# Recurrent layer: the two token tiles go through the doubling levels half a level apart, with the state's products in ten pieces

## The reference, cut to what matters

```python
def wkv7_scan(r, w, k, v, kk, a):          # heads H = 32, N = 64
    def step(state, inp):
        r_t, w_t, k_t, v_t, kk_t, a_t = inp
        sa = jnp.einsum('bhvk,bhk->bhv', state, -kk_t)
        state = (state * w_t[:, :, None, :]
                 + sa[..., None] * (kk_t * a_t)[:, :, None, :]
                 + v_t[..., None] * k_t[:, :, None, :])
        return state, jnp.einsum('bhvk,bhk->bhv', state, r_t)
    ...
    _, out = lax.scan(step, state0, xs)
# odd_layer, around it
    o = wkv7_scan(r, decay, k, v, kk, a)
    o = ((o - mean) * lax.rsqrt(var + GN_EPS)).reshape(B_, S, D) * gn_w + gn_b
    bonus = jnp.sum(r * k * r_k, axis=-1, keepdims=True) * v
    o = (o + bonus.reshape(B_, S, D)) * jax.nn.silu(g)
    return o.astype(x.dtype) @ w_o
```

## Time and profile before

| | |
|---|---|
| median of 3 runs | 2848.18 us (2842.56 to 2848.41) |
| the profiled execution, its own time | 2849.75 us |
| its span in the profile | 2848.0 us |
| PE, DVE, ACT, POOL busy over the whole span | 89%, 53%, 45%, 7% |
| the recurrence, first product of round 0 to the last product of round 8 | about 2401 to 2729 us of the span |

### The profile page before, as it was taken

How to read it: one execution, slowest core, us unless ns; L and a number is a source line. 1 busy time by engine, 2 the same in 40 slices (tenths; PEclk the granted TensorE clock), 3 DMA queues, 4 the chain that set the end, 5 groups by cost and what they waited for, 6 DMA issues and landing times.

```text
span 2848.0 us, 39475 instructions
## 1 busy us (share of the span) xinstructions
PE 2546.3 (89%) x16067; PEld 2112.4 (74%) x16067; DVE 1509.8 (53%) x1914; ACT 1277.8 (45%) x1669; POOL 188.2 (7%) x205
## 2 busy tenths in 40 slices
PE   5999999999699999989997999695999994777785
PEld 4886888878588888878886888584788884666774
DVE  4444554574466666664444444356665543565645
ACT  4434444564455555554444444643354443444332
POOL 1002000000000000000000000000000002243310
PEclk9999999999899999999998999897999996888898
DMA  6655566655355555546554555154466654112052
GB/s 198 194 174 45 178 203 210 205 181 194 130 190 178 180 188 177 177 178 221 192 192 153 193 189 195 45 178 140 163 214 215 221 199 107 49 43 53 14 222 74
DMA packets 231278, 459.27 MB, mean 161 GB/s; under 512 B 9766, under 2 KB 29319, under 8 KB 228844
## 3 DMA queue, kind: packets, MB, share of 16 engines
q1 hardware_dynamic: 221584, 419.99, 44.6%
q0 software_dynamic: 8576, 35.00, 4.7%
q10 hardware_dynamic: 988, 2.41, 0.2%
HBM read 442.64 MB, written 14.71 MB: 161 GB/s over the span
## 4 chain that ended last, share of the span: by engine, by line
PE 41%; DVE 6%; ACT 3%; POOL 2%; issue 2%; DMA 1%; SPq 0%; DVEq 0%; ACTq 0%; POOLq 0%
PE bank L305 12%; PE bank L306 12%; PE bank L307 12%; PE bank L1668 2%; PE bank L1498 1%; DMA raw<-in_od_w_o 1%; PE bank L1724 1%; DVE X L1329 1%; PE bank L1749 1%; DVE d_products L1638 1%; PE bank L1987 0%; DVE d_inverse L1695 0%; PE bank L1520 0%; PE bank L1629 0%; POOL d_t L1572 0%
## 5 line engine op out<-in xcount | busy, mean ns | idle before, releaser
L242 DVE TENSOR_TENSOR w_low<-raw,w_high 128x1024 fp32r<-128x1024 f32 x768 | 930.1, 1219 | 908.0 <-ACT w_high L236 907.3
L236 ACT ACTIVATE w_high<-raw 128x1024 fp32r<-128x1024 f32 x768 | 807.0, 1057 | 988.9 <-PE bank L307 960.1
L305 PE MATMUL bank<-w_high,b_h_high 128*128 128x512 f32 x704 | 277.5, 394 | 8.2 <-DVE w_low L242 5.9
L307 PE MATMUL bank<-w_high,b_h_low 128*128 128x512 f32 x704 | 274.9, 391 | 0.0
L306 PE MATMUL bank<-w_low,b_h_high 128*128 128x512 f32 x704 | 274.7, 390 | 0.0
L305 PE MATMUL bank<-w_high,a_h_high 128*128 128x512 f32 (+1 forms) x640 | 245.8, 384 | 2.1 <-DVE a_bias_rows L754 2.1
L307 PE MATMUL bank<-w_high,a_h_low 128*128 128x512 f32 (+1 forms) x640 | 245.6, 384 | 0.0
L306 PE MATMUL bank<-w_low,a_h_high 128*128 128x512 f32 (+1 forms) x640 | 245.6, 384 | 0.0
L305 PE MATMUL bank<-w_high,d_high 128*128 128x512 f32 x512 | 200.8, 392 | 7.2 <-DVE d_low L2063 7.2
L305 PE MATMUL bank<-w_high,c_x_high 128*128 128x512 f32 x512 | 199.4, 389 | 2.0 <-DVE c_x_low L428 2.0
L307 PE MATMUL bank<-w_high,d_low 128*128 128x512 f32 x512 | 200.2, 391 | 0.0
(11 more groups left out here) (373 smaller groups left out, 3834.0 us busy)
## 6 DMA issues: line engine op xcount, KB each, us to landing
raw<-in_w_up SPq DMA_DIRECT2D x88, 1024.0 KB, 5.1
raw<-in_w_in SPq DMA_DIRECT2D x76, 1024.0 KB, 5.1
raw<-in_ev_w_in SPq DMA_DIRECT2D x48, 1024.0 KB, 5.1
raw<-in_w_down SPq DMA_DIRECT2D x44, 1024.0 KB, 5.0
raw<-in_w_out SPq DMA_DIRECT2D x16, 1024.0 KB, 5.0
raw<-in_ev_w_out SPq DMA_DIRECT2D x16, 1024.0 KB, 5.0
raw<-in_od_w_r SPq DMA_DIRECT2D x16, 1024.0 KB, 5.0
raw<-in_od_w_k SPq DMA_DIRECT2D x16, 1024.0 KB, 5.1
```

The costliest lines, as they stand in the source:

```text
L236: act.activation(wh[n % 4][:, :, 0:width], raw_half, ACT.Copy).then_inc(sem("w_high_made"), 1)
L242: vec.tensor_tensor(wl[n % 4][:, :, 0:width], raw_half, wh[n % 4][:, :, 0:width].bitcast(F32), ALU.subtract).then_inc(sem("w_low_made"), 1)
L305: pe.matmul(b, xh, wh[n][:, k % 2, 0:width], start=(c == 0 and k == 0), stop=False)
L307: mm = pe.matmul(b, xl, wh[n][:, k % 2, 0:width], start=False, stop=(c == j.chunks - 1 and k == 3))
```

## The change

It writes the two tiles of the levels apart. Before, a half level held one stage of both tiles. Now `level_slot(i)` gives for slot i of 0 to 10 a stage of tile 0 and the stage before it of tile 1: slot 0 is Y1 of tile 0, slot 1 T1 of tile 0 and Y1 of tile 1, slot 2 Y2 of tile 0 and T1 of tile 1, and so on to slot 10, T5 of tile 1. The state's step `s` becomes `s0` (chunks 0 and 2) and `s1` (chunks 1 and 3), `o0` becomes `o00` and `o01` (one tile each), and all ten steps get slots of their own. `PREP_AT`, `POST_AT` and `SCORE_AT` are renumbered with the slots; the post steps stand later. Level 0 has a function of its own, `first_level`, at the end of slot 10. The number of products, copies and transposes is the same. The waits change names with the steps (`s` to `s1`, `o0` to `o01`, `rx2` to `rx13`); these lines are left out below.

```diff
--- before.py
+++ after.py
...
-        "state_pe": ["r0", "w", "xq", "s", "p1", "p2", "o0", "ru"],
+        "state_pe": ["r0", "w", "xq", "s0", "s1", "p1", "o00", "p2", "o01", "ru"],
...
-    def level_pe(pe, n, k, stage):
+    def level_pe(pe, n, k, stage, t):
...
+    def first_level(vec, n):
...
-        if step == "s":
-            await_step(pe, "state_act", "xq", n)
-            if n >= 1:
-                await_step(pe, "state_vec", "o1", n - 1)
+        if step in ("s0", "s1"):
+            b = int(step[1])
+            if b == 0:
...
-            for c in (0, 1, 2):
-                t, b = CHUNKS[c]
-                s = half_of(b)
-                for h in range(4):
-                    e = slice(64 * h, 64 * h + 64)
-                    into(c, h, ADD_AT[c], KH[par][s, t, e], v[s, t, e])
-                    into(c, h, ADD_AT[c], NEG_B[par][s, t, e], WW[s, t, e])
-            for c in (1, 2, 3):
-                t, b = CHUNKS[c]
-                s = half_of(b)
+            for t in range(2):
+                c = 2 * t + b
                 for h in range(4):
                     e = slice(64 * h, 64 * h + 64)
                     if c < 3:
-                        into(c, h, PASS_AT[c], XQ[s, t, e], NEG_B[par][s, t, e])
-                    op = into(c, h, READ_AT[c], XQ[s, t, e], mb[t][s, h, 64:128])
+                        into(h, ADD_AT[c], KH[par][s, t, e], v[s, t, e])
+                        op = into(h, ADD_AT[c], NEG_B[par][s, t, e], WW[s, t, e])
+                    if c in (1, 2):
+                        into(h, PASS_AT[c], XQ[s, t, e], NEG_B[par][s, t, e])
+                    if c > 0:
+                        op = into(h, READ_AT[c], XQ[s, t, e], mb[t][s, h, 64:128])
             inc(op)
...
-        if step == "o0":
-            for t in range(2):
+        if step in ("o00", "o01"):
+            t = int(step[2])
+            for kind in range(2):
...
-        if step == "s":
-            await_step(vec, "state_pe", "s", n)
+        if step == "s0":
+            await_step(vec, "state_pe", "s0", n)
             fresh(0)
+            passed(2)
+            reads(0)
+        if step == "s1":
+            await_step(vec, "state_pe", "s1", n)
             passed(1)
             reads(1)
-            passed(2)
-            reads(0)
         if step == "p1":
...
-    STATE_AT = {1: ["r0"], 2: ["w", "xq"], 3: ["s"], 4: ["p1"], 5: ["p2", "o0"], 6: ["ru"]}
-    PREP_AT = {1: 1, 3: 2, 4: 3, 5: 4, 6: 5, 7: 6}
-    POST_AT = {6: 1, 7: 2, 8: 3, 9: 4}
+    STATE_AT = {0: ["r0"], 1: ["w"], 2: ["xq"], 3: ["s0"], 4: ["s1"], 5: ["p1", "o00"], 6: ["p2"], 7: ["o01"], 8: ["ru"]}
+    PREP_AT = {0: 1, 2: 2, 3: 3, 4: 4, 6: 5, 7: 6}
+    POST_AT = {8: 1, 9: 2, 10: 3, 11: 4}
     SCORE_AT = {8: 0, 9: 1}
 
-    def pipeline(eng, level, state, prep, post, score):
+    def level_slot(i):
+        k = (i + 1) // 2
+        if i % 2:
+            return [(k, "T", 0), (k, "Y", 1)]
+        return ([(k + 1, "Y", 0)] if k < 5 else []) + ([(k, "T", 1)] if k else [])
+
+    def pipeline(eng, level, state, prep, post, score, first):
         for part in range(1, 7):
             prep(eng, 0, part)
         for part in range(2):
             score(eng, 0, part)
-        level(eng, 0, 0, "Y")
+        first(eng, 0)
         for n in range(GROUPS + 1):
-            for half in range(1, 11):
-                if n < GROUPS:
-                    level(eng, n, (half + 1) // 2, "TY"[half % 2])
-                if n >= 1 and half in STATE_AT:
-                    for step in STATE_AT[half]:
+            for i in range(12):
+                if n < GROUPS and i < 11:
+                    for k, stage, t in level_slot(i):
+                        level(eng, n, k, stage, t)
+                if n >= 1:
+                    for step in STATE_AT.get(i, ()):
                         state(eng, n - 1, step)
-                if n + 1 < GROUPS and half in PREP_AT:
-                    prep(eng, n + 1, PREP_AT[half])
-                if n >= 1 and half in POST_AT:
-                    post(eng, n - 1, POST_AT[half])
-                if n + 1 < GROUPS and half in SCORE_AT:
-                    score(eng, n + 1, SCORE_AT[half])
-            if n + 1 < GROUPS:
-                level(eng, n + 1, 0, "Y")
+                if n + 1 < GROUPS and i in PREP_AT:
+                    prep(eng, n + 1, PREP_AT[i])
+                if n >= 1 and i in POST_AT:
+                    post(eng, n - 1, POST_AT[i])
+                if n + 1 < GROUPS and i in SCORE_AT:
+                    score(eng, n + 1, SCORE_AT[i])
+                if n + 1 < GROUPS and i == 10:
+                    first(eng, n + 1)
...
```

More of the change, by code:

```diff
@@ new lines, in level_pe @@
+    def level_pe(pe, n, k, stage, t):
+        x = T0[t] if k == 1 else XT[n % 2][t]
+        if stage == "Y":
+            await_step(pe, "level_vec", f"{k - 1}X{t}", n)
+            if k == 1 and n >= 1:
+                await_step(pe, "level_act", f"5T{t}", n - 1)
+        else:
+            await_step(pe, "level_vec", f"{k}Y{t}", n)
+        for h in range(4):
+            for b in range(2):
+                s = slice(64 * b, 64 * b + 64)
+                if stage == "Y":
+                    left, right = MB[n % 2][t][s, h, 0:64], XI[t][s, h, :]
+                else:
+                    left, right = YI[k - 1][t][s, h, :], x[s, h, :]
+                op = pe.matmul(PS[t][s, 64 * h:64 * h + 64], left, right, start=True, stop=True)
+        op.then_inc(sem("level_pe"), 1)
@@ L1785, in state_pe @@
                         e = slice(64 * h, 64 * h + 64)
-                        pe.matmul(PS[3][s, head(t, h)], mk[t][s, h, 64:128], v[s, t, e],
-                                  start=(t == 0 and h == 0), stop=True, skip_group_check=True)
-                for h in range(4):
-                    for b in range(2):
-                        s = half_of(b)
-                        e = slice(64 * h, 64 * h + 64)
-                        op = pe.matmul(PS[3][s, head(t, h)], mb[t][s, h, 64:128], WW[s, t, e],
-                                       start=False, stop=True, skip_group_check=True)
+                        left, right = (mk[t][s, h, 64:128], v[s, t, e]) if kind == 0 else (mb[t][s, h, 64:128], WW[s, t, e])
+                        op = pe.matmul(PS[3][s, head(t, h)], left, right, start=(t == 0 and kind == 0 and h == 0),
+                                       stop=True, skip_group_check=True)
             inc(op)
@@ L1807, in state_act @@
     def state_act(act, n, step):
-        for name, bank, out in (("r0", 2, R0), ("w", 3, WW), ("xq", 2, XQ), ("o0", 3, O0)):
+        for name, bank, out in (("r0", 2, R0), ("w", 3, WW), ("xq", 2, XQ), ("o01", 3, O0)):
             if step == name:
@@ L1847, in state_vec @@
         if step == "ru":
-            await_step(vec, "state_act", "o0", n)
+            await_step(vec, "state_act", "o01", n)
             await_step(vec, "state_pe", "ru", n)
```

103 lines of the change are left out of this document (43 added, 60 removed).

## The result

The changed kernel took 2870.52 us (median of 5 runs, 2868.32 to 2877.03), the kernel before 2848.18 (5 runs on the same chip, 2842.56 to 2856.38): 1.0078 times as long, 95% interval 1.0063 to 1.0094. The forecast was 2866, in a range of 2845 to 2883.

The account below looks back on a forecast made before the run. A chain of prep, score and level 0 through all engines bounds a round, not the doubling levels. Six rounds at +3.5 us give +21, the last rounds -3.5: +17.5 on 2849.75, adjusted to 2866 us; range 2845 to 2883.

Parts of the forecast that it names:

- A: Round's start to prep's row additions: 4.9 us against 6.2, as `r0` follows tile 0's first product directly.
- B: Row additions to prep's reduction of the squares: 5.85 us against 7.9, the VectorE steps of `s` no longer ahead.
- C: Reduction of the squares to first step of prep 3: 4.6 us plus 0.3 for slow products, against 2.9; table load exposed.
- D: First step of prep 3 to `bonus_sum`, the chain GpSimd to VectorE: untouched, 8.5 us.
- E: `bonus_sum` to the next round: 17.25 us at full clock, 19.0 with one slow stretch, against 13.8.
- The three mechanisms: From `bonus_sum` to next round: turns 0 and 1 behind it; `ru`'s additions and post 1 before masks; post's root late.
- the first rival: Lower clock does not meet the long run behind `bonus_sum`: round 40.6 us, +3 in all, 2851; chance 0.18.
- The third rival: Clock stays low over round's start and the run behind `bonus_sum`: 2 to 3 us more per round, 2881; chance 0.20.
- Stalls: Three kinds of wait without a releaser in the six full rounds, 9.1 us together: taken as unchanged.
- the second rival: Faster: TensorE's waits without a releaser, 9.1 us, go, with the lower clock missing the long run: 2842; chance 0.15.
- Round 0: First round of the recurrence, without state or post, 36.28 us before: change of 0, within 2 either way.
- Rounds 7 and 8: Last rounds: 7, without prep, gains 2.7 us from parting; 8 gains 0.8 with `s0`'s VectorE steps beside `s1`.

Follow-up runs that it names:

- the tables alone: New tables and ten state steps of the changed kernel, both tiles side by side in each stage as in the kernel before: 2877.47 us, 1.0102 of the kernel before.
- the filled kernel: Changed kernel plus ten unread 128x256 products per full round, five in each of slots 4 and 10 where TensorE waited: 2856.19 us, 1.0022 of the kernel before.
- `xq` early: Changed kernel with `xq` moved into slot 1, right behind `w`: 2863.27 us, 1.0043 of the kernel before.
- `bonus_sum` late: Changed kernel with `bonus_sum` three slots later, behind turns 2 and 3: 2857.26 us, 1.0026 of the kernel before.
- post behind: Kernel before with post 1 behind half level 9, parts 2 and 3 behind next group's level 0, part 4 in the next round: 2826.08 us, 0.992.

## Why the prediction was right

**The chain.** That the places of the other work decide, and not the levels, holds: the tables alone cost 27 us and the whole change 22, and moving post alone takes 31 off. That parting would give nothing fits as well, since with the old tables it cost 16 us; why it costs that, the prediction did not have. That the levels are never late is argued from these runs, not measured.

**A.** Forecast 4.9, measured 3.6 to 6.6, mean 5.6. Mis-sized on both sides: at full clock it is 3.6 (the filled kernel, in all rounds), since the 1.85 us that I took for `r0` were themselves a row at the low clock (1.10 at full), and it is 5.1 where `r0` is slow, or 6.6 where the low-rank products are slow too (at 2616.15 they take 3.78 us). The low clock thus costs A 1.5 to 3.0 us. The sum came within 0.7 of the mean because the two errors offset.

**B.** Forecast 5.85, measured 5.78.

**C.** Forecast 4.9 with the slow products, measured 5.45 and in two rounds 7.03. The cause is the one named, the table load: with `xq` early it is 4.5. In the two rounds of 7.03 the product of `xq`, for which copy and load wait, meets the low clock (1.86 and 1.65 us, 1.10 in the others); the 0.3 for slow products was too little for that. What was too short is the walk behind the root: `u1` stood 0.74 us for the product of `s0` (2538.99).

**D.** Forecast 8.5, measured 8.36 to 8.89, once 10.93. The missed step: `minus_b` and `key` of the next group wait for `s1`.

**E.** Forecast 17.25 at full clock and 19.0 with one slow stretch, measured 17.42 in two rounds, 17.7 in one, and 19.2 to 19.5 in three. The three mechanisms stand in the rows. The turns behind `bonus_sum` have a run of their own (E 16.9 without, 18.4 with); masks and root behind post have one together (E 14.6). So the two of post are the larger part of E's loss, which the walk did not say, and which of them counts for more no run parts.

**The sum of a round.** 43.1 and a longer A in most, +3.5, measured 44.7 and +3.8; six rounds +22.6 against +21. Mean against mean the +3.8 are A -1.0, B -2.8, C +2.3, D +0.5, E +4.8. The forecast's base was one clean round, in which B and C too were under the mean of the six (7.9 and 2.9, mean 8.6 and 3.7), and not only A.

**The clock.** I gave it 1.75 us of E and 0.5 of A. The filled kernel is 2.7 us a round faster, 0.6 of it in D by waits without a releaser that are gone: the rest is about the size I gave the clock, but it is in A and not in E, which is still 17.6 to 19.2 there. At full clock the walk gave 2851 (the first rival); with the products that hold the clock up 2856 was measured. The third rival (2881) wanted the low clock over the start and the run of E in each round: A is 6.6 in three rounds and E over 19 in the three others, and no round has both.

**Stalls.** Forecast unchanged, 9.1 us; measured 4.5 + 2.9 = 7.4, while the second rival needed over 60% of them gone. TensorE's waits without a releaser in the six rounds, the answer to the earlier trace rows:

```profile
PE bank L1750 <- issue: 4.5, 2, 2.3
PE bank L1666 <- issue: 2.9, 1, 2.9
```

**Round 0.** Forecast 0 within 2, measured +2.1. The failing term is its last stretch, 14.0 from `bonus_sum` on and not 11.2; before it was 11.9. With `bonus_sum` late round 0 took 33.3, so turns behind it cost here as they do in the others. **Rounds 7 and 8.** Forecast -2.7 and -0.8, together measured -1.5: round 7 gained 2.0 (22.3 us), and round 8 lost about 0.5 where a gain was forecast. These two errors, +2.1 and +2.0, the 1.6 in the rounds and the 1.5 behind them are offset in the profiled execution by the 6.0 us by which it began the recurrence early; by its median the kernel is 4.5 above the forecast. So the total is nearer than its terms, and part of that is luck. Of the signs that the prediction named, three were overrun: the round (44.7, not 42 to 44), A (mean 5.6, not 4.4 to 5) and, in three rounds, E (over 19).

What stays open: why the parted kernel's round stays longer even where post is out of the way (37.55 us against 34.6). By stretches it is longer in C (5.5 against 2.9, the table load) and E (14.4 against 10.9, the turns still behind `bonus_sum`) and shorter in A and B, so the tables have a part in it; moving `xq` and the turns shortened both and brought A up again. Open too is why from round 7 on several parted kernels take 38 to 41.5 us to the last output and others 34. No run isolates either.

## What to carry to other kernels

Before a finer pipelining of a stage is built, find whether that stage is late; here it had, by the prediction's estimate, 14 us of 39, and what counted most was which short, waiting steps stood on VectorE's queue ahead of the step that opens the next round. Work that only leads to an output (here post: a sum, a root with its table load, a norm) belongs behind that step: moved so, it was worth 23 to 25 us in the old kernel and 31 in the new, more than the parting lost. And a duration read from a row at TensorE's low clock must not be summed as if the new order would meet the same clock: take it at both levels and carry both.

## What the hardware showed

Filling TensorE's waits with unread products made the changed kernel 0.56% faster, and did nothing for the one before, whose unread products did not reach the slow ones at a round's start (above). The Trainium skill (TensorE: Matmul & The Clock Gate, "HAM oscillation — how this bites in real kernels") has the clock fall in kernels that work in short bursts between waits. The traces agree in part: the granted clock of the changed kernel's six rounds is 0.82 with the waits and 0.93 with two of them filled, but behind the same wait of 2.32 us `r0` took 1.10 us in one run and 1.78 in another.

VectorE's second masked copy of level 0 took 1.00 us beside GpSimd and 0.41 without. In the changed kernel the one at 2567.85 (VectorE) starts during a product of GpSimd:

```profile
2567.17 1.38 POOL L1932 TENSOR_TENSOR d_o<-d_o,d_norm_rows_of 128x512 f32<-128x512 f32 x1 [17.72 <-DVE d_o L1922]
```

GpSimd's ends at 2568.55, the copy 0.30 later. The Trainium skill (SBUF — State Buffer, "🔬 SBUF: two separate sides") says that of a VectorE instruction with two operands from SBUF and a GpSimd one, the first to start holds the shared ports to its end. The trace agrees here. In the six rounds the level 0 masks have these means (VectorE, count, busy us, mean ns), before and with post behind in the same kernel:

```profile
L1687 DVE COPY_PREDICATED d_first<-d_tables,d_products 128x256 f32<-128x256 int32 x13 | 10.6, 815 | 0.0
```

```profile
L1687 DVE COPY_PREDICATED d_first<-d_tables,d_products 128x256 f32<-128x256 int32 x13 | 5.4, 418 | 0.0
```
